# Weighted one-hot rows on GpSimd, and one filler product with VectorE sums in the step between layers

## The chip, the cores and the metric

The program runs on one core of a Trainium2 chip. A core has TensorE (matrix products, with its own weight loads), VectorE, ScalarE, GpSimd and SyncE, which here only issues DMAs. They run side by side and meet at semaphores. The metric is the device time of one execution in microseconds (us); lower is better.

## The reference

Two transformer blocks of two layers each, one after the other, on 256 tokens of width 1024, all in float32. This case touches two pieces.

The first block's feed-forward part is a product-key mixture (PEER), once per layer. Each token picks 16 of 16,384 experts in each of 8 heads, so 128 (expert, gate) pairs a token:

```python
def peer_ffn(h, w_q, sub_keys, u, v):
    scores = einsum('bshpd,hpnd->bshpn', (h @ w_q).reshape(b, s, 8, 2, 128), sub_keys)
    s1, i1 = top_k(scores[..., 0, :], 16); s2, i2 = top_k(scores[..., 1, :], 16)
    cand = s1[..., :, None] + s2[..., None, :]          # 256 candidates a head
    top, pos = top_k(cand, 16); gates = softmax(top)    # expert = (i1, i2) at pos
    act = gelu(einsum('td,ted->te', h, u[expert]))
    return einsum('te,ted->td', gates * act, v[expert])
```

The second block adds each sublayer's normed result, `x = x + g * rmsnorm(y, gain)`, and norms the new `x` again at the entry of the next sublayer.

## The kernel before

**The expert sublayer (`peer`).** No expert row is gathered. All 16,384 experts are treated densely, as 128 units of 128 experts (`KEYS` = 128), each a 128x1024 block of `u` that comes by DMA into a ring of 4 slots. For exact float32 products a unit is split into a high and a low part: ScalarE writes the high part (`high`, L2403), VectorE the low part (`low`, L2264), and TensorE multiplies 24 times (`hidden`, L2475) into PSUM. Three split buffers (`SPLITS`) tie them: ScalarE may make unit u's high part only when TensorE is done with unit u-3. ScalarE then applies the gelu (L2411) and SyncE stores the result.

In the same loop the routing is worked out. VectorE finds the top 16 in `top16` (max, max_index, match_replace) and turns the candidates into (first key, second key, gate) for the token half 1 and then for half 0. `pace()` puts a `low()` between the pieces of this work, five times in six. At the end of each half TensorE transposes the three lists (`turn`, L2483) and VectorE copies them to `selT` (L2385).

A dense table of gates, `G[key1, token, key2]`, is then built by products of one-hot rows. A batch is 4 tokens (`B` = 4), and there are 64 batches a layer. For each token VectorE makes a row `(iota == key1) * gate` (L2288, 4 instructions a batch) and, in one instruction for all four, `(iota == key2)` (L2291); TensorE multiplies each pair (`place`, L2493), and ScalarE copies the result into `G` (`take`, L2428). Both kinds of rows have two buffers, so batch n waits until `place(n-2)` is done. The order is fixed when the program is written: 16 batches of token half 1 are made between the routing steps of half 0 (`pace`, every second unit), the other 48 after both halves, one with each unit. TensorE's queue holds `hidden(j)`, then `turn` or `place` where VectorE's count says so, then `hidden(j+1)`.

**The step between sublayers of the second block (`add_streamed`).** It runs four times; in three of them (`counted`) it also sums the squares of the new `x`. TensorE sums the squares of `y` over partitions (L863), then multiplies seven times into a bank that nobody reads (L866, fillers), and widens the inverse roots (L869), which VectorE needs for `y * root` (L899) and `x + y` (L903), in four quarters. ScalarE squares each quarter (L916), and TensorE sums all the squares with 32 one-column products (16 with 256 columns; L876). At the next entry VectorE adds the four quarter sums (L144) and forms the root.

## Time and profile before

| | |
|---|---|
| three runs | median 3641.14 us (3630.91 to 3643.29) |
| the profiled execution | 3646.81 us, its span 3645.1 us |
| mean granted TensorE clock | 0.942 of full speed |
| TensorE busy | 3344.1 us, 92% |
| VectorE busy | 2173.9 us, 60% |
| ScalarE busy | 1453.5 us, 40% |
| GpSimd busy | 41.6 us, 1% |
| the expert sublayers' loop over `u` | about 455 to 890 us and 1480 to 1915 us |
| the four steps between sublayers | at 2794, 3207, 3388 and 3629 us |

The span runs from the first to the last instruction; the 1.7 us beside it lie around it. Busy shares are means over stages with different limits, so the place of an idle stretch and what ended it say more than the share. A `x4` in a row is several instructions in one; its time then runs from the first start to the last end, and instructions on one engine overlap a little at their ends.

### The profile page before, as it was taken

The numbers are of one execution on the slowest core, as the hardware profiler recorded it, in microseconds if no ns is written. First come the engines' busy times: TensorE is split into PE (matmuls) and PEld (weight loads), VectorE is DVE, ScalarE is ACT, GpSimd is POOL, SyncE is SP. The second block draws the span as 40 slices with busy tenths as digits, with TensorE's granted clock in tenths as the row PEclk, the third lists the DMA queues.
The fourth block names the chain that finished last, engine by engine and source line by source line (L and its number), as shares of the span: only waits on it lengthen the run. The fifth ranks groups of instructions, "written<-read, shape, count | busy, mean of one in ns | idle before, by whom it ended". The sixth has DMA issues, their size and how long they took to land. (4 is left out here: it accounts for less than half of the span.)

```text
span 3645.1 us, 54606 instructions
## 1 busy us (share of the span) xinstructions
PE 3344.1 (92%) x20704; PEld 2871.6 (79%) x20704; DVE 2173.9 (60%) x4205; ACT 1453.5 (40%) x2254; POOL 41.6 (1%) x66
## 2 busy tenths in 40 slices
PE   6987899999999798999999999799789999979897
PEld 4844799998888678999997887577556787867897
DVE  4523489875787635799767787423673443244553
ACT  3312444444455434444444544332233322233443
POOL 0000000000000000000000000000020000000000
PEclk7987999999999899999999999799897999979899
DMA  5465576556888635666567886322551232311353
GB/s 182 148 230 189 185 212 202 173 174 190 243 240 243 201 107 168 203 197 183 176 183 229 241 243 212 121 83 93 195 185 41 85 94 92 94 56 49 114 168 121
DMA packets 225066, 596.62 MB, mean 164 GB/s; under 512 B 27424, under 2 KB 97440, under 8 KB 224576
## 3 DMA queue, kind: packets, MB, share of 16 engines
q1 hardware_dynamic: 220656, 588.17, 52.6%
q10 hardware_dynamic: 4176, 5.29, 0.5%
q8 instruction: 152, 2.49, 0.3%
q14 instruction: 82, 0.67, 0.1%
HBM read 558.16 MB, written 35.19 MB: 163 GB/s over the span
## 5 line engine op out<-in xcount | busy, mean ns | idle before, releaser
L2475 PE MATMUL ps<-h_split,split_layer 128*128 128x256 f32 x6144 | 773.3, 285 | 11.0 <-DVE split_layer L2264 11.0
L2475 PEld LDWEIGHTS ps<-h_split,split_layer 128*128 128x128 f32 x6144 | 746.7, 192 | 14.3 <-DVE split_layer L2264 14.3
L2621 PE MATMUL ps<-split_layer,h_split 128*128 128x512 f32 x3072 | 702.3, 392 | 13.8 <-DVE h_split L2605 13.8
L2621 PEld LDWEIGHTS ps<-split_layer,h_split 128*128 128x128 f32 x3072 | 580.6, 189 | 135.1 <-DVE split_layer L2588 14.2
L784 PE MATMUL ps<-h_parts_ffn,split_ffn 128*128 128x512 f32 (+1 forms) x2112 | 381.6, 342 | 14.8 <-DVE split_ffn L736 8.2
L784 PEld LDWEIGHTS ps<-h_parts_ffn,split_ffn 128*128 128x128 f32 x2112 | 331.5, 193 | 65.8 <-issue 17.0
L2264 DVE TENSOR_TENSOR split_layer<-ring,split_layer 128x1024 fp32r<-128x1024 f32 x256 | 311.8, 1220 | 79.6 <-ACT split_layer L2403 77.9
L2588 DVE TENSOR_TENSOR split_layer<-ring,split_layer 128x1024 fp32r<-128x1024 f32 x256 | 313.7, 1226 | 0.0
L736 DVE TENSOR_TENSOR split_ffn<-ring,split_ffn 128x1024 fp32r<-128x1024 f32 x132 | 161.1, 1225 | 253.9 <-ACT split_ffn L711 245.9
L2411 ACT ACTIVATE kept_layer<-ps 128x256 f32<-128x256 f32 x256 | 98.3, 384 | 459.3 <-PE ps L2475 459.2
L2570 ACT ACTIVATE split_layer<-ring 128x1024 fp32r<-128x1024 f32 x256 | 267.6, 1045 | 4.5 <-PEq L472 4.5
L2403 ACT ACTIVATE split_layer<-ring 128x1024 fp32r<-128x1024 f32 x256 | 268.8, 1051 | 0.7 <-PEq L472 0.7
L2579 ACT ACTIVATE h_split<-x_sb 128x256 fp32r<-128x256 f32 x256 | 107.2, 419 | 350.2 <-PE ps L2621 345.8
L784 PE MATMUL ps<-hidden_ffn,split_ffn 128*128 128x512 f32 (+1 forms) x1056 | 189.4, 342 | 11.3 <-DVE split_ffn L736 11.3
L711 ACT ACTIVATE split_ffn<-ring 128x1024 fp32r<-128x1024 f32 x132 | 136.0, 1056 | 150.2 <-PE ps L784 125.0
L2605 DVE TENSOR_TENSOR h_split<-x_sb,h_split 128x256 fp32r<-128x256 f32 x256 | 109.2, 427 | 141.5 <-ACT h_split L2579 141.5
L784 PEld LDWEIGHTS ps<-hidden_ffn,split_ffn 128*128 128x128 f32 x1056 | 166.2, 194 | 34.5 <-issue 10.7
L2288 DVE TENSOR_SCALAR x_sb<-small 128x128 f32<-128x128 f32 x512 | 142.8, 343 | 84.7 <-PE ps L2493 84.6
L2597 DVE TENSOR_TENSOR x_sb<-x_sb,routes_layer 128x256 f32<-128x256 f32 x256 | 161.0, 629 | 21.4 <-DMA x_sb<-hidden_layer 21.4
L784 PE MATMUL ps<-h_parts_recurrent,split_recurrent_in 128*128 128x512 f32 x576 | 135.3, 396 | 9.3 <-DVE h_parts_recurrent L280 8.1
L784 PEld LDWEIGHTS ps<-h_parts_recurrent,split_recurrent_in 128*128 128x128 f32 x576 | 108.8, 190 | 36.2 <-issue 7.3
L2493 PE MATMUL ps<-x_sb 128*128 128x128 f32 x1024 | 136.9, 277 | 0.0
(612 smaller groups left out, 3891.1 us busy)
## 6 DMA issues: line engine op xcount, KB each, us to landing
ring<-in_experts SPq DMA_DIRECT2D x512, 512.0 KB, 3.9
ring<-in_mod SPq DMA_DIRECT2D x96, 512.0 KB, 4.6
ring<-in_ada SPq DMA_DIRECT2D x96, 512.0 KB, 4.4
ring<-in_ffn_in SPq DMA_DIRECT2D x88, 512.0 KB, 3.5
hidden_layer<-kept_layer SPq DMA_DIRECT2D x256, 128.0 KB, 2.0
x_sb<-hidden_layer SPq DMA_DIRECT2D x256, 128.0 KB, 3.9
ring<-in_ffn_out SPq DMA_DIRECT2D x44, 512.0 KB, 3.6
ring<-in_peer_q SPq DMA_DIRECT2D x32, 512.0 KB, 3.6
```

Of the source, the lines that this page charges most:

```text
L711: nc.scalar.activation(split[:, s % slots, 0, :], self.slot(u0 + s), ACT.Copy).then_inc(hi_done.sem, 1)
L736: nc.vector.tensor_tensor(split[:, s % slots, 1, :], self.slot(u0 + s), split[:, s % slots, 0, :].bitcast(F32), ALU.subtract).then_inc(sel ...
L784: ins = nc.tensor.matmul(ps[:, m % BANKS, 0:n], a, b, start=(k == 0 and j == 0), stop=(k == kt - 1 and j == 2))
L2264: v.tensor_tensor(split[:, u % SPLITS, 1, :], self.slot(unit0 + u), split[:, u % SPLITS, 0, :].bitcast(F32), ALU.subtract).then_inc(self.u ...
L2288: v.tensor_scalar(row1(half, j), self.iota, sel[:, 0, t:t + 1], sel[:, 2, t:t + 1], ALU.is_equal, ALU.mult)
L2403: s.activation(split[:, u % SPLITS, 0, :], self.slot(unit0 + u), ACT.Copy).then_inc(hi_done.sem, 1)
L2475: ins = nc.tensor.matmul(ps[:, 4 + j % 2, 0:T], w[:, part, c], self.hsplit[:, moving, k, :], start=(k == 0 and n == 0), stop=(k == KT - 1 ...
L2493: ins = nc.tensor.matmul(ps[:, n % 2, j * P:(j + 1) * P], row1(n % 2, j), row2(n % 2, j), start=True, stop=True)
L2570: s.activation(split[:, u % SPLITS, 0, :], self.slot(unit0 + u), ACT.Copy).then_inc(hi_done.sem, 1)
L2588: v.tensor_tensor(split[:, u % SPLITS, 1, :], self.slot(unit0 + u), split[:, u % SPLITS, 0, :].bitcast(F32), ALU.subtract).then_inc(self.u ...
L2597: v.tensor_tensor(raw(j), held(j), G[:, :, j:j + 1].rearrange("p t o -> p (t o)"), ALU.mult).then_inc(weighed_j.sem, 1)
L2621: ins = nc.tensor.matmul(ps[:, 2 * t + h, :], wsplit(j, a)[:, t * P:(t + 1) * P], w[:, b, h * 512:(h + 1) * 512], start=(j == 0 and n == 0 ...
```

## The change

In `peer`, the four weighted rows of a batch are no longer made by VectorE. GpSimd makes them, all 64 batches in a queue of its own: it waits for the list of the half (a semaphore of its own, raised by VectorE's copy to `selT`), and from the third batch on for `place(n-2)`. VectorE still makes the `(iota == key2)` rows of all four tokens, at the same places. TensorE's `place(n)` waits for both. In `add_streamed` one filler stands where seven stood; in the counted steps three fillers come after the last squares, VectorE adds the eight blocks of squares to one (four instructions), and TensorE's 32 (or 16) one-column products become 4 (or 2). The entry no longer adds quarter sums.

```diff
@@ class Norm, vector_root @@
-        if self.counted:
-            v.tensor_reduce(self.root, ps[:, 5, 16:16 + 4 * self.nt].rearrange("p (i t) -> p t i", t=self.nt), AX_X, ALU.add
-                            ).then_inc(done.sem, 1)
-            dve.wait_ge(done.sem, done.up())
-            v.tensor_scalar(self.root, self.root, 1.0 / D, EPS, ALU.mult, ALU.add).then_inc(done.sem, 1)
-        else:
-            v.tensor_scalar(self.root, ps[:, 5, 0:self.nt], 1.0 / D, EPS, ALU.mult, ALU.add).then_inc(done.sem, 1)
+        at0 = 16 if self.counted else 0
+        v.tensor_scalar(self.root, ps[:, 5, at0:at0 + self.nt], 1.0 / D, EPS, ALU.mult, ALU.add).then_inc(done.sem, 1)
@@ add_streamed, TensorE @@
-                for i in range(7):
-                    mm(ps[:, 7, 0:T], self.ones, total[:, 0:T], start=True, stop=True)
+                mm(ps[:, 7, 0:T], self.ones, total[:, 0:T], start=True, stop=True)
...
                 if counted:
-                    for i in range(QUARTERS):
-                        pe.wait_ge(self.squared.sem, at[self.squared] + i + 1)
-                        for t in range(nt):
-                            for k in range(per):
-                                ins = mm(ps[:, 5, 16 + i * nt + t:17 + i * nt + t],
-                                         squares[:, i * per + k, t * P:(t + 1) * P], self.ones[:, 0:1],
-                                         start=(k == 0), stop=(k == per - 1))
+                    pe.wait_ge(self.squared.sem, at[self.squared] + QUARTERS)
+                    for i in range(3):
+                        mm(ps[:, 7, 0:T], self.ones, total[:, 0:T], start=True, stop=True)
+                    pe.wait_ge(folded.sem, at[folded] + QUARTERS)
+                    for t in range(nt):
+                        ins = mm(ps[:, 5, 16 + t:17 + t], squares[:, 0, t * P:(t + 1) * P], self.ones[:, 0:1],
+                                 start=True, stop=True)
@@ add_streamed, VectorE, at the end of round i of the quarters @@
+                    if counted and i >= 3:
+                        dve.wait_ge(self.squared.sem, at[self.squared] + i - 1)
+                        if i > 3:
+                            dve.wait_ge(folded.sem, at[folded] + i - 3)
+                        a, b = fold(i - 2)
+                        v.tensor_tensor(a, a, b, ALU.add).then_inc(folded.sem, 1)
+                if counted:
+                    dve.wait_ge(self.squared.sem, at[self.squared] + QUARTERS)
+                    dve.wait_ge(folded.sem, at[folded] + QUARTERS - 2)
+                    a, b = fold(QUARTERS - 1)
+                    v.tensor_tensor(a, a, b, ALU.add).then_inc(folded.sem, 1)
+                    dve.wait_ge(folded.sem, at[folded] + QUARTERS - 1)
+                    v.tensor_tensor(squares[:, 0, :], squares[:, 0, :], squares[:, 1, :], ALU.add).then_inc(folded.sem, 1)
@@ peer, the loop over u @@
+            @block.gpsimd
+            def _(pool):
+                for n in range(BATCHES):
+                    half, b = n % 2, BATCH_ORDER[n]
+                    if n % (BATCHES // 2) == 0:
+                        pool.wait_ge(chosen.sem, chosen.n + n // (BATCHES // 2) + 1)
+                    if n >= 2:
+                        pool.wait_ge(placed.sem, placed0 + n - 1)
+                    for j in range(B):
+                        t = b * B + j
+                        ins = nc.gpsimd.tensor_scalar(row1(half, j), self.iota, sel[:, 0, t:t + 1], sel[:, 2, t:t + 1],
+                                                      ALU.is_equal, ALU.mult)
+                    ins.then_inc(weighted.sem, 1)
@@ onehot_rows, VectorE @@
-                    for j in range(B):
-                        t = b * B + j
-                        v.tensor_scalar(row1(half, j), self.iota, sel[:, 0, t:t + 1], sel[:, 2, t:t + 1],
-                                        ALU.is_equal, ALU.mult)
@@ the copy to selT, VectorE @@
-                                  ps[:, 6, 0:3 * P].rearrange("p (a b) -> p a b", a=3)).then_inc(done.sem, 1)
-                    after()
+                                  ps[:, 6, 0:3 * P].rearrange("p (a b) -> p a b", a=3)).then_inc(chosen.sem, 1)
+                    dve.wait_ge(chosen.sem, chosen.n + i + 1)
@@ place(n), TensorE @@
                     pe.wait_ge(onehots.sem, onehots0 + n + 1)
+                    pe.wait_ge(weighted.sem, weighted0 + n + 1)
```

VectorE's order in the later 48 batches of the first layer, before: one batch and one `low` a unit. `handover_k` is raised by `place`, `handover_a` by ScalarE's high part; `x_sb<-small` is a row made from the lists.

```order
L2288 TENSOR_SCALAR x_sb<-small 128x128 [waits handover_k]
L2288 TENSOR_SCALAR x_sb<-small 128x128 x3
L2291 TENSOR_TENSOR x_sb<-small 128x2x256
L2264 TENSOR_TENSOR split_layer<-ring,split_layer 128x1024 [waits handover_a]
L2288 TENSOR_SCALAR x_sb<-small 128x128 [waits handover_k]
```

The same place in the changed kernel, where L2320 is the row for four tokens and L2297 the low part:

```order
L2320 TENSOR_TENSOR x_sb<-small 128x2x256 [waits handover_k]
L2297 TENSOR_TENSOR split_layer<-ring,split_layer 128x1024 [waits handover_a]
L2320 TENSOR_TENSOR x_sb<-small 128x2x256 [waits handover_k]
L2297 TENSOR_TENSOR split_layer<-ring,split_layer 128x1024 [waits handover_a]
L2320 TENSOR_TENSOR x_sb<-small 128x2x256 [waits handover_k]
```

Four rows a batch are gone from VectorE, and its wait for `place(n-2)` has passed to the remaining row. GpSimd's order in the changed kernel, at the same place, with the rows in its own queue:

```order
L2285 TENSOR_SCALAR x_sb<-small 128x128 [waits handover_k]
L2285 TENSOR_SCALAR x_sb<-small 128x128 x3
L2285 TENSOR_SCALAR x_sb<-small 128x128 [waits handover_k]
L2285 TENSOR_SCALAR x_sb<-small 128x128 x3
```

TensorE keeps its order there; only the first product of a batch (L2524 in the changed kernel) has one more semaphore to wait for.

```order
L2524 MATMUL ps<-x_sb 128x128 [waits handover_l,weighted_rows,handover_j]
L2524 MATMUL ps<-x_sb 128x128 x3
L2504 MATMUL ps<-h_split,split_layer 128x256 [waits handover_c,unit_used]
L2504 MATMUL ps<-h_split,split_layer 128x256 x23
```

TensorE's order in the first of the four steps between sublayers, before:

```order
L863 MATMUL ps<-small,arena_block_layer 128x1 x4
L866 MATMUL ps<-arena_block_layer,small 128x256 x7
L869 MATMUL ps<-arena_block_layer,small 128x512
L876 MATMUL ps<-small,arena_block_layer 128x1 x32
```

and after the change:

```order
L859 MATMUL ps<-small,arena_block_layer 128x1 x4
L861 MATMUL ps<-arena_block_layer,small 128x256
L864 MATMUL ps<-arena_block_layer,small 128x512
L869 MATMUL ps<-arena_block_layer,small 128x256 x3
L873 MATMUL ps<-small,arena_block_layer 128x1 x4
```

Six fillers have left the place ahead of the widening product, three have come behind it, and 28 of the 32 one-column products are gone.

## Rows read from the trace of the kernel before

**Rows 1.** The page, busy time, share of the span and instructions.

```profile
PE 3344.1 (92%) x20704; PEld 2871.6 (79%) x20704; DVE 2173.9 (60%) x4205; ACT 1453.5 (40%) x2254; POOL 41.6 (1%) x66
```

**Rows 2.** Busy time by stretches: length, then engines' busy us, granted clock, DMA share, GB/s.

```profile
700.00:720.00 20.00, 20.00 (x172) 20.00 (x172) 15.34 (x31) 9.16 (x16) 0.00 (x0) 1.00 0.58 184
```

**Rows 3.** Timeline of one unit among the later batches: start, length, engine, line.

```profile
704.66 1.06 PE L2493 MATMUL ps<-x_sb 128*128 128x128 f32 x8
705.76 1.12 DVE L2288 TENSOR_SCALAR x_sb<-small 128x128 f32<-128x128 f32 x4 [0.91 <-PE ps L2493]
706.79 0.68 DVE L2291 TENSOR_TENSOR x_sb<-small 128x512 f32<-128x512 f32 x1
707.40 1.21 DVE L2264 TENSOR_TENSOR split_layer<-ring,split_layer 128x1024 fp32r<-128x1024 f32 x1
708.43 1.06 PE L2493 MATMUL ps<-x_sb 128*128 128x128 f32 x8
```

**Rows 4.** Timeline where the routing of half 0 ends, first layer.

```profile
665.32 1.23 DVE L2264 TENSOR_TENSOR split_layer<-ring,split_layer 128x1024 fp32r<-128x1024 f32 x1
666.46 1.12 DVE L2288 TENSOR_SCALAR x_sb<-small 128x128 f32<-128x128 f32 x4
666.60 3.14 PE L2475 MATMUL ps<-h_split,split_layer 128*128 128x256 f32 x24 [0.34 <-DVE split_layer L2264]
673.29 0.29 DVE L2379 TENSOR_TENSOR routes_layer<-routes_layer 128x128 f32<-128x128 f32 x1
673.64 0.90 PE L2483 MATMUL ps<-small,routes_layer 128*128 128x128 f32 x3 [3.90 <-DVE routes_layer L2379]
674.34 1.92 PE L2493 MATMUL ps<-x_sb 128*128 128x128 f32 x8
```

**Rows 5.** TensorE's turn, L2483: its idle time ahead, weight loads and products, both layers.

```profile
  DVE routes_layer L2379: 16.0, 4
```

**Rows 6.** Busy time of L2288 alone: length, VectorE busy (instructions), clock, DMA.

```profile
540.00:672.00 132.00, 17.78 (x64) 1.00 0.64 192
```

**Rows 7.** The page, ScalarE's high part: busy us, mean ns, idle before.

```profile
L2403 ACT ACTIVATE split_layer<-ring 128x1024 fp32r<-128x1024 f32 x256 | 268.8, 1051 | 0.7 <-PEq L472 0.7
```

**Rows 8.** GpSimd's instructions by form: busy us, mean ns.

```profile
L3099 POOL TENSOR_TENSOR arena_recurrent<-arena_recurrent,arena_block_layer 128x512 f32<-128x512 f32 x7 | 8.9, 1268 | 0.0
L1218 POOL TENSOR_SCALAR_AFFINE_SELECT small<-small 128x128 f32<-128x128 f32 x8 | 2.4, 300 | 0.6
```

**Rows 9.** Lines where GpSimd runs beside VectorE: min/median/max ns.

```profile
L1218 POOL TENSOR_SCALAR_AFFINE_SELECT arena_layer<-arena_layer x2: 1158/1158/1159, 55.5 to 56.7; 128x128 f32<-128x128 f32 x2
L1819 DVE TENSOR_TENSOR h_split<-h_layer,h_split x2: 1227/1270/1312, 54.0 to 55.2; 128x1024 fp32r<-128x1024 f32 x2
```

**Rows 10.** Timeline, the recurrent stage, VectorE beside GpSimd's L3100.

```profile
2620.44 1.75 DVE L3133 TENSOR_TENSOR arena_recurrent<-arena_recurrent,arena_block_layer 128x512 f32<-128x512 f32 x1
```

**Rows 11.** Timeline of the first step between sublayers.

```profile
2797.68 5.96 PE L866 MATMUL ps<-arena_block_layer,small 128*128 128x256 f32 x14
2798.50 0.87 DVE L891 TENSOR_SCALAR arena_block_layer<-small,arena_block_layer 128x128 f32<-128x128 f32 x4 [0.27 <-ACT arena_block_layer L910]
2803.48 1.02 PE L869 MATMUL ps<-arena_block_layer,small 128*128 128x512 f32 x2
2804.54 2.35 DVE L899 TENSOR_TENSOR h_block_layer<-h_block_layer,ps 128x1024 f32<-128x1024 f32 x2 [5.16 <-PE ps L869]
2809.17 13.81 PE L876 MATMUL ps<-small,arena_block_layer 128*128 128x1 f32 x64 [4.67 <-ACT arena_block_layer L916]
2812.59 2.19 ACT L916 ACTIVATE arena_block_layer<-x_sb 128x1024 f32<-128x1024 f32 x2 [1.21 <-DVE x_sb L903]
2825.91 0.17 DVE L144 TENSOR_REDUCE entry_ffn<-ps 128x4 f32<-128x16 f32 x1
```

**Rows 12.** Busy time by stretches, the fillers of the same step.

```profile
2800.00:2802.00 2.00, 2.00 (x6) 1.64 (x5) 0.00 (x0) 0.00 (x0) 0.00 (x0) 0.50 0.00 0
```

**Rows 13.** VectorE's L899, its idle time ahead over all four steps.

```profile
  PE ps L869: 16.2, 4
```

More of the change, by code:

```diff
@@ L436, in __init__ @@
          self.l) = (sig(f"handover_{x}") for x in "abcdefghijkl")
+        self.gates_chosen, self.weighted_rows = sig("routes_chosen"), sig("weighted_rows")
         self.kept = [sig(f"hidden_kept{i}") for i in range(2)]
@@ L852, in add_streamed @@
         x = self.xT[:, :, c0:c1]
-        scaled, summed = self.a, self.c
+        scaled, summed, folded = self.a, self.c, self.e
         counts, inverted, rooted, diagonals, widened = (self.entry_counted, self.inverted, self.rooted, self.diagonals,
@@ L857, in add_streamed @@
         per = KT // QUARTERS
-        at = {s: s.n for s in (scaled, summed, counts, inverted, rooted, diagonals, widened, self.squared)}
+        at = {s: s.n for s in (scaled, summed, folded, counts, inverted, rooted, diagonals, widened, self.squared)}
         with self.block() as block:
@@ L896, in _ @@
                 part = lambda i: slice(i * per, (i + 1) * per)
+                fold = (lambda i: (squares[:, part(0), :], squares[:, part(i), :])) if counted else None
                 for i in range(QUARTERS + 1):
@@ L920, in add_streamed @@
         if counted:
-            self.squared.up(QUARTERS)
+            self.squared.up(QUARTERS), folded.up(QUARTERS)
         self.arena.at = mark
@@ L2253, in peer @@
         gate_at, found_at, place_at = [], [], []
+        chosen, weighted = self.gates_chosen, self.weighted_rows
+        weighted0 = weighted.n
         with self.block() as block:
+            @block.gpsimd
[11 more added lines that the diff above has]
+                    ins.then_inc(weighted.sem, 1)
             @block.vector
@@ L2527, in peer @@
             x.up(TT)
-        for x in (onehots, placed, taken):
+        for x in (onehots, placed, taken, weighted):
             x.up(BATCHES)
+        chosen.up(TT)
         for x in self.kept:
```

## Prediction

> **What bounds the kernel now.** I read the page's busy times first: TensorE is busy for 92% of the span, GpSimd for 1% [rows 1]. So a change on VectorE or GpSimd is worth only what TensorE waits for them, and that is read stage by stage. Next the busy time by stretches. Where the later batches are made TensorE is busy for 20.00 of 20 us and VectorE for 15.34 [rows 2]. The timeline of one unit there says the same: `place` starts at 704.66 and again at 708.43, a period of 3.77 us; VectorE finds its buffer free only when a `place` ends, after 0.91 us idle [rows 3]. VectorE waits for TensorE, not the reverse. Then the end of the routing of half 0: VectorE is never idle, TensorE waits 0.34 and then 3.90 us for it, and the eight records of the `place` behind the last wait take 1.92 us where they take 1.06 in the steady state [rows 3, 4]. The second layer has the same last wait: the four idle times (weight loads and products, two layers) add to 16.0 us [rows 5]. Last the step between sublayers, which is a serial chain: whatever leaves it shortens the program. Its fillers run at half the granted clock, 1.2 GHz [rows 12].
>
> **Part 1, the rows leave VectorE, later batches (48 a layer).** VectorE loses four instructions, 1.03 us from the first start to the start of L2291 [rows 3]. TensorE has no wait there, so this is worth nothing; TensorE's 3.77 us hide it. VectorE keeps 0.68 and 1.21 us a unit [rows 3].
>
> The added wait is TensorE's, for GpSimd's rows. Behind it in TensorE's queue stands the next `hidden`, and behind that everything. GpSimd is released by `place(n-2)`, at 705.72, and its rows are wanted by `place(n)`, one unit after 708.43, at 712.2: 6.5 us. Over many batches it must keep to 3.77 us for four instructions. No row shows this instruction on GpSimd. The nearest is a select over 128x128 with one tensor input, 0.30 us; the far end is a 128x512 sum with two, 1.27 us [rows 8]. Mine has the small shape, but two operations and two per-partition scalars: I take 0.5 us, near the first, so 2.0 us a batch.
>
> It also meets VectorE. Beside back-to-back low parts of the same shape as L2264, GpSimd's select took 1.158 instead of 0.30 us: it got in only between VectorE's instructions. VectorE's instruction took 1.312 instead of 1.227 us, 0.085 more [rows 8, 9]. With two inputs of 512 elements GpSimd held up VectorE longer: L3133, a 128x512 sum that takes 0.68 us beside nothing, took 1.75 [rows 10]. So one side waits while the other reads, and a read of 128 elements is short. In a unit, then: GpSimd's first instruction ends behind L2291, at about 0.8 us, the second behind L2264, at 2.0, and two free ones at 3.0: under 3.77. TensorE's period then stays. If no part of GpSimd's work overlapped VectorE's 1.9 us, the batch would take 3.9: 0.13 us over, 6 us in 48 batches, of which the 2.7 us in hand (6.5 less 3.77) absorb part. I take nothing; the ends are 0 and 7 us later over both layers.
>
> The Trainium skill (SBUF — State Buffer, section Who interferes with whom) says that a VectorE instruction with two SBUF inputs and a GpSimd instruction that reads SBUF exclude each other, and that the second blocks fully. The trace agrees for GpSimd's wait [rows 9]; for VectorE it shows a price of 0.085 us, not of an instruction. The sum by the rule taken whole is my third rival.
>
> The skill's GPSIMD Engine Reference (section Engine selection) puts GpSimd at about half VectorE's speed for two-input elementwise work and near its speed for one input. By it the four rows would take an estimated 1.4 to 2.7 us, which fits in 3.77 and changes no term.
>
> **Part 2, the same in the routing of half 0 (16 batches a layer, 64 instructions [rows 6]).** Here VectorE is the late one. A batch frees 1.03 us and GpSimd costs at most 4 x 0.085 = 0.34, net 0.7; 16 batches give 11 us. VectorE can't use them all, since the low part of unit u needs the high part, and that needs `hidden(u-3)` to be over. How far ahead must it be? After its last low part ahead of the `turn` (665.32 + 1.23 = 666.55) VectorE works until 673.58 [rows 4]; 7.0 less 0.7 is 6.3 us, and TensorE needs 3.1 for that unit's `hidden`, so a lead of 3.2 us at 666.55 closes the gap. The greatest lead is two `hidden` and a `place`, 2 x 3.1 + 1.06, less what stands between the end of `hidden(u-3)` and the low part of u: a gelu, 1.05 for the high part [rows 7] and 1.21 [rows 3], in all about 2.9. That is 4.4 us, enough by 1.2 if lumps of 2.3 us in VectorE's work don't use it up. TensorE then gains 0.34 + 3.90 and the slow restart, 1.92 - 1.06 = 0.9: 5.1 a layer, 10.3 for both [rows 4, 5]. I take 10; the ends are -31 (VectorE loses, the third rival) and 11. The first rows are early: GpSimd may start them at the copy to `selT`, ahead of VectorE's next search. Here GpSimd has two units a batch (over 6.6 us), so a wait behind a 2.3 us instruction is covered. No DMA is moved; the fetch of a unit follows its low part, a few us earlier, with TensorE still behind.
>
> **Part 3, six fillers leave (four steps).** In the first step seven fillers take 5.96 us from 2797.68, though VectorE's diagonals are ready at 2798.50 + 0.87 = 2799.37 [rows 11]. One filler takes 0.85 and ends before them. So VectorE's wait ahead of L899, 5.16 us there and 16.2 over the four steps [rows 11, 13], shrinks to the widening product: 1.02 us for 512 columns after the clock had risen [rows 11], twice that at 1.2 GHz, half that for 256 columns. Without fillers I expect the low level in the two wide steps: 2.1 + 2.1 + 1.0 + 0.9 = 6.1. Gain 10.1 us; with all four at the low level 9.4, at the high level 12.5.
>
> **Part 4, sums of squares (three steps).** First step, counted from the start of L899 at 2804.54. Before: L876 ends at 2822.98, 18.4 us. After: the last square, 10.2 us in [rows 11], moves by one VectorE addition, 1.13, to 11.4. Two more additions on VectorE end at 13.3; the three fillers, at 0.85, end at 13.9 and decide; 8 records of 64, 13.81/8 = 1.7, end at 15.7. Gain 2.7, and the same in the second. In the third everything but the fillers is half as long: 9.2 before, 5.7 + 2.6 + 0.9 = 9.2 after, nothing. Together I take 5 us. With fillers at the high clock 1.3 us a step and half the products go too, up to 10; were the additions slower than the fillers, 2.
>
> **Part 5.** L144 and the wait behind it go from the entry chain, 0.2 us three times [rows 11]: 0.6.
>
> **Sum.** 10 + 10.1 + 5 + 0.6 = 25.7 us. The profiled execution took 3646.8 (span 3645.1), 5.7 over the median of the runs; it would take 3621. From the median, 3641.1 - 25.7 = 3615.
>
> **Rivals.**
> - *GpSimd sets the pace* (slower). For: one half of the bounds lies there; the instruction has no row. It decides from 0.47 us an instruction without any overlap with VectorE, from 0.94 with full overlap (3.77/4). Priced at 0.9 us with half of VectorE's 1.9 us in the way: 4.55 a batch, 0.78 over, times 48, less 2.7 in hand: 35 us a layer, 70 in all. The routing's gain goes as well: 70 - 15.7 = +54, 3695. Against: 0.30 us for the nearest form. Chance 0.10.
> - *The routing's gain doesn't come*, because VectorE's lead is used up in lumps or TensorE waits for GpSimd's rows there. Gain 15.7 to 18: 3624. For: the margin is 1.2 us against lumps of 2.3. Chance 0.15.
> - *Each GpSimd instruction holds VectorE up for its whole 0.5 us.* Then a batch in the routing costs VectorE 2.0 against 1.03 freed: 16 us later a layer, 31 in all, and the later batches 3.9 us each, some 7. 38 - 15.7 = +22: 3663. For: L3133 was held up for 1.07 us [rows 10]. Against: 0.085 for the small shape. Chance 0.04.
> - *The clock.* The fillers that leave are TensorE's only wide work in the step, and its entry and first products then run at 1.2 GHz for some us longer. Four places at 2 to 4 us: gain 10 to 16, 3628. Against: at 2809 to 2823 TensorE was busy with L876 and the next products started at the low level already. Chance 0.15, of which 0.06 falls within 0.3%.
> - *Nothing to be told apart*, by small losses at each wait: 3640. Chance 0.04.
>
> **How the numbers follow.** The forecast has 0.52; its own range is 3603 to 3623: with every part at its good end the sum is 34 us, 3607, and the runs before spread over 12 us. 0.3%, 11 us, is about what a measurement of this kernel can tell from no change. Faster: 0.52 + 0.15 + 0.09 = 0.76. Within: 0.06 + 0.04 = 0.10. Slower: 0.14. The range runs from 3603 to 3644; it leaves out the slower cases and a little below.
>
> **What would show it.** Right: GpSimd's rows near 0.5 us between VectorE's, 2 to 3.1 us a batch; the period in the later batches still 3.77; TensorE's wait ahead of L2483's successor for half 0 under 0.8 instead of 3.90; VectorE's waits ahead of `y * root` adding to about 6 instead of 16.2; 15.7 from there to the last one-column product in the first step. Wrong: a period over 3.8 with TensorE waiting for GpSimd, VectorE's L2264 longer by more than 0.1 us each, or a granted clock of half speed for longer behind the steps.

## The result: slower by 1.1%

The changed kernel takes 3680.45 us (median of 3 runs, 3675.05 to 3680.94) against 3641.14: ratio 1.0108, 95% interval 1.0087 to 1.0130. The forecast was 3615 in a range of 3603 to 3644, a gain; it became a loss. The profiled execution took 3680.94 us, its span 3679.2, mean granted clock 0.946.

### The profile page after: what moved, and what is told of

Same layout as the page of the kernel before. It is cut to its first block and busy times, and to the rows that moved or that the text cites. A ratio compares the mean times of both kernels' runs of the same rounds, so it can differ in the third digit from the quotient of the medians.

```text
span 3679.2 us, 54287 instructions
## 1 busy us (share of the span) xinstructions
PE 3323.3 (90%) x20534; PEld 2839.4 (77%) x20534; DVE 2057.6 (56%) x3702; ACT 1453.5 (40%) x2254; POOL 622.0 (17%) x578
## 5 line engine op out<-in xcount | busy, mean ns | idle before, releaser
L2285 POOL TENSOR_SCALAR x_sb<-small 128x128 f32<-128x128 f32 x512 | 580.3, 1147 | 899.7 <-DVE small L2414 823.9
L780 PE MATMUL ps<-h_parts_ffn,split_ffn 128*128 128x512 f32 (+1 forms) x2112 | 381.9, 342 | 15.9 <-DVE split_ffn L732 8.2
L2297 DVE TENSOR_TENSOR split_layer<-ring,split_layer 128x1024 fp32r<-128x1024 f32 x256 | 313.1, 1225 | 109.3 <-ACT split_layer L2432 108.0
L2320 DVE TENSOR_TENSOR x_sb<-small 128x512 f32<-128x512 f32 x128 | 88.5, 691 | 235.7 <-PE ps L2524 235.6
L780 PEld LDWEIGHTS ps<-hidden_ffn,split_ffn 128*128 128x128 f32 x1056 | 167.4, 195 | 34.1 <-issue 10.3
L2524 PE MATMUL ps<-x_sb 128*128 128x128 f32 x1024 | 142.5, 282 | 39.8 <-issue 39.8
L2524 PEld LDWEIGHTS ps<-x_sb 128*128 128x128 f32 x1024 | 125.3, 192 | 55.1 <-issue 55.1
```

The source lines that it names most:

```text
L780: ins = nc.tensor.matmul(ps[:, m % BANKS, 0:n], a, b, start=(k == 0 and j == 0), stop=(k == kt - 1 and j == 2))
L2285: ins = nc.gpsimd.tensor_scalar(row1(half, j), self.iota, sel[:, 0, t:t + 1], sel[:, 2, t:t + 1], ALU.is_equal, ALU.mult)
L2297: v.tensor_tensor(split[:, u % SPLITS, 1, :], self.slot(unit0 + u), split[:, u % SPLITS, 0, :].bitcast(F32), ALU.subtract).then_inc(self.u ...
L2524: ins = nc.tensor.matmul(ps[:, n % 2, j * P:(j + 1) * P], row1(n % 2, j), row2(n % 2, j), start=True, stop=True)
```

## The profile after

The page's busy times and two of its costliest groups, to be set beside [rows 1, 7]. The last column of a group is the idle time of the engine ahead of it.

```profile
PE 3323.3 (90%) x20534; PEld 2839.4 (77%) x20534; DVE 2057.6 (56%) x3702; ACT 1453.5 (40%) x2254; POOL 622.0 (17%) x578
...
L2285 POOL TENSOR_SCALAR x_sb<-small 128x128 f32<-128x128 f32 x512 | 580.3, 1147 | 899.7 <-DVE small L2414 823.9
...
L2524 PE MATMUL ps<-x_sb 128*128 128x128 f32 x1024 | 142.5, 282 | 39.8 <-issue 39.8
```

GpSimd took over 512 instructions and is busy 580 us more. TensorE now has 39.8 us of idle time ahead of `place` (L2524), with no instruction of the profile named for it ("issue"). What it waits for is seen among the later batches. Busy time by stretches, to be set beside [rows 2]:

```profile
700.00:720.00 20.00, 17.77 (x143) 17.10 (x144) 7.93 (x10) 9.07 (x15) 20.00 (x20) 1.00 0.48 143
```

GpSimd, the fifth of the busy columns, is busy for 20.00 of 20 us and TensorE no longer. The timeline of one unit, to be set beside [rows 3]:

```profile
699.52 11.24 POOL L2285 TENSOR_SCALAR x_sb<-small 128x128 f32<-128x128 f32 x11
...
704.86 1.13 PE L2524 MATMUL ps<-x_sb 128*128 128x128 f32 x8 [0.46 <-issue]
...
706.02 0.69 DVE L2320 TENSOR_TENSOR x_sb<-small 128x512 f32<-128x512 f32 x1 [2.62 <-PE ps L2524]
706.63 1.22 DVE L2297 TENSOR_TENSOR split_layer<-ring,split_layer 128x1024 fp32r<-128x1024 f32 x1
...
709.31 0.91 PE L2524 MATMUL ps<-x_sb 128*128 128x128 f32 x6 [0.45 <-issue]
```

`place` starts at 704.86 and 709.31: a period of 4.45 us instead of 3.77. GpSimd never stops, and VectorE idles 2.62 us a unit instead of 0.91. GpSimd is the engine with no slack. Its instruction by itself (min/median/max ns), over the later batches, and then the one that runs at 706.9 to 707.0 in the unit above:

```profile
L2285 POOL TENSOR_SCALAR x_sb<-small x117: 783/789/2150, 719.7 to 848.7; 128x128 f32<-128x128 f32 x117
L2285 POOL TENSOR_SCALAR x_sb<-small x1: 2147/2147/2147, 706.3 to 706.3; 128x128 f32<-128x128 f32 x1
```

Three of the four instructions of a batch take 0.79 us. One is 2.15 us long: it starts at 706.3, while VectorE's L2320 runs (from 706.02), and ends at 708.4, some 0.6 us behind the end of L2297 (707.85). It is held up for 2.15 - 0.79 = 1.36 us. Together 3 x 0.79 + 2.15 = 4.5 us, the period of 4.45, since neighbours overlap a little.

The hidden products of each layer give the length of the loop (first and last start stand ahead of the form). Before, then after, in both layers:

```profile
L2475 PE MATMUL ps<-h_split,split_layer x3072: 278/283/562, 443.0 to 885.8; 128*128 128x256 f32 x192
L2475 PE MATMUL ps<-h_split,split_layer x3072: 278/283/561, 1469.7 to 1912.6; 128*128 128x256 f32 x192
```

```profile
L2504 PE MATMUL ps<-h_split,split_layer x3072: 277/283/415, 435.8 to 904.5; 128*128 128x256 f32 x192
L2504 PE MATMUL ps<-h_split,split_layer x3072: 277/283/561, 1486.8 to 1958.1; 128*128 128x256 f32 x192
```

The first loop began at 443.0, not at about 455 as the table of before has it. The loops lasted 442.8 and 442.9 us and now last 468.7 and 471.3: +54.3 together. The steps between sublayers give back 14.0 (worked out below). The span grew by 34.1; the remaining -6.2 is mostly the time ahead of the first loop, which began at 443.0 before and at 435.8 after. No part of the change lies there, and in the kernels below that start varies from 429.6 to 443.7, so I don't count it as an effect of the change.

The end of the routing of half 0, to be set beside [rows 4]:

```profile
663.67 0.55 PE L2512 MATMUL ps<-small,routes_layer 128*128 128x128 f32 x3 [2.87 <-DVE routes_layer L2408]
664.05 1.06 PE L2524 MATMUL ps<-x_sb 128*128 128x128 f32 x8
```

The wait for the finished lists is 2.87 us, neither the old 3.90 nor the expected value under 0.8. The first step between sublayers, to be set beside [rows 11]:

```profile
2843.22 1.61 PE L859 MATMUL ps<-small,arena_block_layer 128*128 128x1 f32 x8 [2.48 <-PEq L468]
2844.69 1.20 PE L861 MATMUL ps<-arena_block_layer,small 128*128 128x256 f32 x2
2846.45 2.08 PE L864 MATMUL ps<-arena_block_layer,small 128*128 128x512 f32 x2 [0.55 <-DVE arena_block_layer L887]
2859.99 2.93 PE L869 MATMUL ps<-arena_block_layer,small 128*128 128x256 f32 x6 [11.47 <-ACT arena_block_layer L931]
2862.71 1.71 PE L873 MATMUL ps<-small,arena_block_layer 128*128 128x1 f32 x8
2865.06 3.78 PE L160 MATMUL ps<-x_sb,small 128*128 128x256 f32 x8 [0.65 <-DVE small L749]
2868.91 2.04 PE L181 MATMUL ps<-scaled_ffn,small 128*128 128x512 f32 x2
...
2873.86 1.32 PE L780 MATMUL ps<-h_parts_ffn,split_ffn 128*128 128x512 f32 x3 [2.91 <-DVE h_parts_ffn L278]
```

VectorE's `y * root` (L896) in that step, and then its idle time ahead over the four steps, to be set beside [rows 13]:

```profile
2848.56 2.35 DVE L896 TENSOR_TENSOR h_block_layer<-h_block_layer,ps 128x1024 f32<-128x1024 f32 x2 [2.17 <-PE ps L864]
```

```profile
  PE ps L864: 5.9, 4
```

The one filler ends at 2845.89, ahead of the diagonals. The widening product takes 2.08 us. VectorE's wait over the four steps fell from 16.2 to 5.9. From the start of L896 at 2848.56 to the end of the last one-column product at 2864.42 it is 15.9 us, where it was 18.4.

## The experiments

Theory A: GpSimd sets the pace of the later batches, by its own 0.79 us an instruction and by being held up behind VectorE's two-input instructions. There are two rivals: that TensorE's added wait and the longer chain cost the time, whatever GpSimd has to do; or that the step between sublayers is what lost. "Loops" below are the lengths of the two loops over `u`, read as above. All kernels were measured against the kernel before on the same chip (its medians: 3641.5 to 3644.5 us); intervals are 95%.

### The rows on GpSimd alone, and the step alone

gpsimd_only is the changed kernel with the old `add_streamed` and the old root at the entry; step_only is the kernel before with the new ones.

> The changed kernel with the step between sublayers and the entry's root as before: GpSimd's rows alone. Theory A (GpSimd sets the pace of the later batches: 0.79 us an instruction, one of four held up 1.36 us behind VectorE's two, 4.45 us a batch against 3.77): the two loops over u are 54 us longer, the rest is as before; 3641 + 54 = 3695 us, ratio 1.015. Theory B (the step between sublayers cost time, GpSimd's rows only a little): ratio under 1.005.

Measured: 3693.16 us, ratio 1.0130 (1.0107 to 1.0154); loops 471.6 and 470.2 us.

> The kernel before with the changed step between sublayers and nothing on GpSimd. Theory A: the step is faster by what its parts showed, some 16 us: 3625 us, ratio 0.9955. Theory B: slower than before, ratio over 1.003.

Measured: 3633.28 us, ratio 0.9966 (0.9950 to 0.9982), loops 442.7 and 443.8 us. So the whole loss is the rows', and the step is worth some 12 us (7 to 18). The sum of both, 1.013 x 0.9966 = 1.0096, is the changed kernel's ratio within its interval.

### GpSimd only in the routing

The first piece stands in GpSimd's queue, the second in VectorE's, the third in TensorE's.

```diff
-                for n in range(BATCHES):
+                for n in range(16):
...
+                    if n >= 16:
+                        for j in range(B):
+                            t = b * B + j
+                            v.tensor_scalar(row1(half, j), self.iota, sel[:, 0, t:t + 1], sel[:, 2, t:t + 1],
+                                            ALU.is_equal, ALU.mult)
...
-                    pe.wait_ge(weighted.sem, weighted0 + n + 1)
+                    if n < 16:
+                        pe.wait_ge(weighted.sem, weighted0 + n + 1)
```

> The changed kernel, but GpSimd makes only the 16 batches of a layer that fall into the routing; VectorE makes the rows of the other 48, as before. Theory A: the later batches are back at 3.77 us, the routing keeps what it gained (TensorE waits some 2.9 instead of 3.9 us ahead of its turn, and restarts without the slow place): 3641 - 16 - 5 = 3620 us, ratio 0.994. Theory C (any work that GpSimd does beside VectorE costs the loop): ratio over 0.9955, the step's gain alone.

Measured: 3622.95 us, ratio 0.9941 (0.9918 to 0.9963), loops 439.8 us both. With the 48 later batches back on VectorE the loss is gone. Against theory C the total alone doesn't decide, as its interval takes in 0.9955; the loops do, being 3.0 us shorter than before. That is the gain in the routing a layer, where the prediction had 5. The profile of this kernel shows why, in the low part's row over the routing (530 to 660 us), and what waited ahead of it:

```profile
L2297 DVE TENSOR_TENSOR split_layer<-ring,split_layer x39: 1199/1224/1389, 530.6 to 658.3; 128x1024 fp32r<-128x1024 f32 x39
...
  ACT split_layer L2437: 11.5, 15
```

VectorE waits 11.5 us, 15 times, for ScalarE's high part. In the kernel before it waited not once over the same stretch of the loop (543 to 672 us, as the loop began 13.4 us later). Its freed time is spent on waiting. By the order of the semaphores it is the three split buffers that cap its lead; no run here changes their number. Beside GpSimd the low part's median is 1.224 us, where before it was 1.217, so the 0.085 us that [rows 9] suggest is not paid each time, though the longest reached 1.389.

### Part of the rows on GpSimd

half_share gives GpSimd two of the four rows of every batch, three_share three; VectorE makes the others (`range(B)` becomes `range(2)` on GpSimd, and VectorE has a loop over `range(2, B)`; for three_share likewise with 3). All waits of the changed kernel stay.

> The changed kernel, but of the four rows of a batch GpSimd makes two and VectorE two. Theory A: GpSimd needs 2 x 0.79 + 1.36 = 2.9 us a batch, under 3.77, so TensorE sets the pace again: 3641 - 16 - 4 = 3621 us, ratio 0.994. Theory D (what costs is TensorE's additional wait for a second engine, 0.45 us idle ahead of each place, whatever GpSimd has to do): the period stays at 4.4 us, ratio 1.01.

Measured: 3621.98 us, ratio 0.9937 (0.9914 to 0.9960), loops 441.5 and 439.0 us.

> The changed kernel, but GpSimd makes three of the four rows of a batch and VectorE one. Theory A (time of a batch on GpSimd = number of rows x 0.79 us + 1.36 us held up behind VectorE): 3.73 us, just under TensorE's 3.77, so the loop is as fast as with two rows: first to last product of the first expert loop 439 to 444 us, ratio 0.993 to 0.996. If the held-up time grows with the number of rows (rows take turns with VectorE's instructions, 0.34 each), 3.4 us, the same. If TensorE's added wait itself cost, the period would be near 4.2 us and the loop near 460 us.

Measured: 3624.19 us, ratio 0.9948 (0.9930 to 0.9966), loops 440.2 us both. TensorE's `place` in half_share, then GpSimd and VectorE in one unit, and GpSimd's instruction over the later batches:

```profile
741.40 1.06 PE L2528 MATMUL ps<-x_sb 128*128 128x128 f32 x8
742.22 3.12 PE L2508 MATMUL ps<-h_split,split_layer 128*128 128x256 f32 x24
745.17 1.06 PE L2528 MATMUL ps<-x_sb 128*128 128x128 f32 x8
```

```profile
742.50 0.66 DVE L2321 TENSOR_SCALAR x_sb<-small 128x128 f32<-128x128 f32 x2 [1.38 <-PE ps L2528]
742.56 2.91 POOL L2285 TENSOR_SCALAR x_sb<-small 128x128 f32<-128x128 f32 x2 [0.85 <-PE ps L2528]
743.08 0.68 DVE L2324 TENSOR_TENSOR x_sb<-small 128x512 f32<-128x512 f32 x1
743.68 1.21 DVE L2297 TENSOR_TENSOR split_layer<-ring,split_layer 128x1024 fp32r<-128x1024 f32 x1
```

```profile
L2285 POOL TENSOR_SCALAR x_sb<-small x66: 862/1441/2065, 720.0 to 841.3; 128x128 f32<-128x128 f32 x66
```

In half_share the period is 3.77 us and TensorE has no wait, though it still waits for the semaphore of GpSimd's rows: the semaphore and the longer chain cost nothing, which rules the first rival out. It also parts the two prices. GpSimd's first instruction lies beside VectorE's one-input rows and takes 0.86 us, hardly more than 0.79. The second meets the two two-input instructions, from 743.08 to 744.89, and takes 2.07: it ends at 745.47, 0.58 us behind the second one's end. It was not let in at the seam between them (743.7), while the select of [rows 9] got in between two low parts; why they differ, no run here shows. With three rows GpSimd is at the edge: busy without a break, with the period still at 3.77 us (three_share):

```profile
740.00:760.00 20.00, 20.00 (x172) 20.00 (x171) 11.52 (x16) 9.09 (x15) 20.00 (x16) 1.00 0.54 167
```

### Shorter hold-up, shorter instruction

key_single is the changed kernel with VectorE's one two-input instruction for the four keys (L2320, 0.69 us) put back into four with one input each:

```diff
-                    v.tensor_tensor(rows2(half), iota4, column_key.unsqueeze(3).broadcast_to([P, B // 2, 2, P]),
-                                    ALU.is_equal).then_inc(onehots.sem, 1)
+                    for j in range(B):
+                        t = b * B + j
+                        ins = v.tensor_scalar(row2(half, j), self.iota, sel[:, 1, t:t + 1], None, ALU.is_equal)
+                    ins.then_inc(onehots.sem, 1)
```

> The changed kernel, but VectorE makes the four (iota == key2) rows with four instructions of one tensor input each in place of one instruction with two. GpSimd makes all four weighted rows. Theory A (only VectorE's instructions with two inputs in SBUF hold GpSimd up, and two of them back to back hold it up for their whole length): only the low part, 1.22 us, is left; the held-up time falls from 1.36 to 0.7 to 0.9 us, the period from 4.45 to 3.8 to 4.05 us, the loop from 469 to 445 to 452 us. Theory G (any VectorE instruction on SBUF holds it up): VectorE is busy for longer, the period grows to 4.8 us or more.

Measured: 3643.05 us, ratio 1.0001 (0.9988 to 1.0015); loops 451.7 and 450.6.

```profile
L2285 POOL TENSOR_SCALAR x_sb<-small x129: 783/989/1543, 719.7 to 849.5; 128x128 f32<-128x128 f32 x129
```

```profile
741.59 1.13 PE L2525 MATMUL ps<-x_sb 128*128 128x128 f32 x8
...
745.65 1.13 PE L2525 MATMUL ps<-x_sb 128*128 128x128 f32 x8
```

Period 4.06. GpSimd still makes all four rows; the longest took 1.54 instead of 2.15 us, 0.6 less, though others were stretched to 0.99. The expectation had put the period at 3.8 to 4.05 us; this is its far end. So 0.39 of the 0.68 us that the period had grown were the hold-up behind that one instruction, worth 17 and 21 us of the loops.

one_op leaves the gate multiplication out of GpSimd's instruction (`sel[:, 2, ...]` and `ALU.mult` become `None`), so its table of gates holds ones:

> The changed kernel, but GpSimd's instruction only compares (one per-partition scalar, one operation); the multiplication by the gate is left out, so the result is not the weighted one. Theory H (the instruction is long because of its second scalar and second operation): it falls from 0.79 to about 0.5 us, 4 x 0.5 + 1.36 = 3.4 us a batch, and the loop is back at TensorE's pace, 440 us, ratio 0.994. Theory I (the length is that of any such instruction on GpSimd): 0.79 stays, period 4.45, ratio 1.01.

Measured: 3619.08 us, ratio 0.9934 (0.9917 to 0.9952), loops 439.5 and 439.6 us.

```profile
L2285 POOL TENSOR_SCALAR x_sb<-small x136: 596/599/2047, 718.5 to 846.0; 128x128 f32<-128x128 f32 x136
```

The second operation with its own scalar costs 0.19 of the 0.79 us. Without it four rows just fit into the 3.77 us, with the hold-up no smaller (2.05 - 0.60 = 1.45). So the hold-up alone is borne. That 0.79 us an instruction alone would be borne too follows from 4 x 0.79 = 3.16 us, under 3.77; no run has it. Both together were not borne.

### One filler, nothing else

one_filler is the kernel before with `for i in range(7)` removed ahead of the filler, so that one is left.

> The kernel before with one filler in place of seven in the step between sublayers and nothing else. Theory A: VectorE's wait ahead of y * root falls from 16.2 to 6 us over the four steps; the rest of the step stays: 3641 - 10 = 3631 us, ratio 0.997. Theory J (the fillers pay for themselves through the clock): the products behind run at 1.2 GHz for longer and the gain is under 3 us, ratio over 0.999.

Measured: 3629.10 us, ratio 0.9963 (0.9946 to 0.9980), not to be told from step_only. Theory J (under 3 us) falls. The profiles part the two kernels. TensorE's timeline in its first and third steps (one filler stands at L865):

```profile
2791.71 1.62 PE L863 MATMUL ps<-small,arena_block_layer 128*128 128x1 f32 x8 [2.48 <-PEq L472]
...
2824.25 5.86 PE L784 MATMUL ps<-h_parts_ffn,split_ffn 128*128 128x512 f32 x12 [2.91 <-DVE h_parts_ffn L283]
...
3379.15 0.58 PE L863 MATMUL ps<-small,arena_block_layer 128*128 128x1 f32 x4 [1.63 <-PEq L472]
...
3384.52 6.99 PE L875 MATMUL ps<-small,arena_block_layer 128*128 128x1 f32 x32 [2.64 <-ACT arena_block_layer L915]
...
3398.38 3.85 PE L784 MATMUL ps<-h_parts_ffn,split_ffn 128*128 128x256 f32 x14 [1.73 <-DVE h_parts_ffn L283]
```

From the first product of the step to the first of the next matrix, in us (step 2 to the first entry product, step 4 to the end of the widening product), before, in one_filler and in the changed kernel:

| step | before | one filler | after |
|---|---|---|---|
| 1 | 35.6 | 32.5 | 30.6 |
| 2 | 33.0 | 30.9 | 27.9 |
| 3 | 21.7 | 19.2 | 19.2 |
| 4 | 4.1 | 2.7 | 2.7 |
| gain | | 9.1 | 14.0 |

The columns sum to 94.4, 85.3 and 80.4 us. Other profiles give the same: 94.7 in gpsimd_only with the old step, and within 0.1 of 80.4 in step_only and key_single with the new one.

### What kept the routing's gain small

TensorE's last wait there stayed at 2.87 us in the changed kernel and in early_gpsimd alike. more_low is early_gpsimd with one more low part ahead of VectorE's last long instructions of half 0; before_more_low is the kernel before with the same, and nothing on GpSimd.

```diff
                         after()
                         pace()
+                        if i == 1 and side == 1:
+                            low()
                         v.tensor_tensor(oh4, oh4, idxs[:, side].unsqueeze(2).broadcast_to(full), ALU.mult).then_inc(done.sem, 1)
```

> The kernel in which GpSimd makes only the rows of the 16 routing batches, with one more low part on VectorE in the last stretch of half 0's routing, ahead of the last multiplication by the expert lists. There TensorE waited 2.87 us for the finished lists (654.46 to 657.33), because VectorE worked from 651.3 to 657.2 without giving it a unit. Theory A (the lead is lumpy: what TensorE lacks is one more unit, not VectorE's time): the added low part takes 1.22 us, the lists are ready at 658.4 instead of 657.2, TensorE has 3.1 us more to do, so its wait falls from 2.87 to about 0.7, the loop from 439.8 to about 437.6 us a layer, the total by some 4 us to 3618, ratio 0.993. Rival B (VectorE's lead is capped by ScalarE's high part, or the sequence simply has too much VectorE work): the added low part waits, or TensorE waits elsewhere for the same time; loop 439.8, ratio 0.994. The two totals can hardly be told apart; the wait and the loop length in the profile decide.

> The kernel before with the same one more low part there, and nothing on GpSimd. Theory A: TensorE's wait ahead of the turn falls from 3.90 to about 1.9 us (hidden product until 672.9, lists at 674.8), the loop from 442.8 to about 440.8 us a layer, ratio 0.999, which a measurement of the total can't tell from 1. Rival B: loop 442.8. If A holds, two thirds of what GpSimd's rows gave in the routing (3.0 us a layer) were to be had by the order alone.

Measured: more_low 3617.76 us, ratio 0.9939 (0.9923 to 0.9955), loops 436.7 us both; before_more_low 3635.88 us, ratio 0.9986 (0.9975 to 0.9997), loops 441.1 us both. The totals can't tell the two theories apart; the profiles do. TensorE's wait ahead of the lists, in more_low and in before_more_low:

```profile
666.26 0.55 PE L2519 MATMUL ps<-small,routes_layer 128*128 128x128 f32 x3 [0.24 <-DVE routes_layer L2415]
```

```profile
675.52 0.55 PE L2485 MATMUL ps<-small,routes_layer 128*128 128x128 f32 x3 [1.28 <-DVE routes_layer L2381]
```

Some 6 us of work that VectorE does there without giving TensorE a unit (651.2 to 657.2 in early_gpsimd) caused the last wait. The order takes 2.6 us off it with the rows on GpSimd (2.87 to 0.24) and without (3.90 to 1.28); freed time on VectorE had taken 1.0 us off it. The loop became shorter by another 3.1 us on top of the 3.0 by rows on GpSimd, but by only 1.7 without them. The difference is the granted clock behind the wait, here by stretches in more_low and then in before_more_low:

```profile
664.00:668.00 4.00, 3.17 (x25) 2.73 (x25) 3.90 (x6) 1.82 (x3) 0.00 (x0) 1.00 0.10 37
676.00:680.00 4.00, 3.41 (x18) 3.35 (x18) 3.96 (x9) 0.09 (x1) 0.00 (x0) 0.63 0.56 143
```

At a clock of 1.00 the next 48 records of `hidden` take 6.02 us, at 0.63 they take 7.51.

### The pieces that help, together

combined is more_low with the old step and one filler.

> What the runs so far point to: GpSimd makes the rows of the 16 routing batches alone, VectorE has one more low part ahead of the last multiplication, and in the step between layers one filler stands where seven stood, with the 32 one-column products and the reduce of the kernel before (no sums on VectorE, no later fillers). Theory A (the step's gain is the fillers', 3629/3642; the sums on VectorE give nothing; the loop gives 5 us a layer): 13 + 10 = 23 us off, 3619, ratio 0.9935, as more_low or within 3 us of it. Rival (the sums on VectorE were worth their 5 us): 5 us slower than more_low, ratio 0.995.

Measured: 3620.64 us, ratio 0.9942 (0.9925 to 0.9959); loops 436.7 us both. It lies 2.9 us above more_low, in the direction of the rival's 5, which runs that spread over 14 and 15 us can't settle. The profiles settle it for the steps: combined needs 85.3 us in the four, as one_filler does, and more_low 80.3, so the sums on VectorE are worth some 4.9 us there, with the loops alike. more_low has the lowest median of all, 0.6% ahead of the kernel before; early_gpsimd, half_share, three_share, one_op and combined can't be told from it.

## Why the prediction was wrong, point by point

**What bounds the kernel** was right: TensorE without a wait in the later batches, VectorE late in the routing.

**Part 1 failed, and with it the sign.** The term that was put at nothing is GpSimd's pace in the later batches ("I take nothing"); it cost some 60 us over both layers. Two steps of the prediction led there. The first is "I take 0.5 us, near the first, so 2.0 us a batch". The second is "a read of 128 elements is short", from which two free instructions and two let in between VectorE's were to end at 3.0 us. The instruction takes 0.79 us, and it isn't let in between: one in four stands 1.36 us behind VectorE's pair. 3.16 + 1.36 = 4.5 us instead of 3.0. The prediction's other estimate for the four rows, 1.4 to 2.7 us, was below the 3.16 as well. The prediction knew both edges (0.47 us an instruction without any overlap, 0.94 with full overlap), and the truth lay between them: of VectorE's 1.83 us only 0.47 overlapped. The first rival, priced at 4.55 us a batch, had the mechanism and nearly the period, 4.45, though with 0.9 us an instruction and a hold-up of 0.95, where 0.79 and 1.36 were measured. Its +35 us a layer were 30.1, and its 3695 for the whole change, which gave up the routing's gain, was 15 us too high. A chance of 0.10 for it rested on the 0.30 us of another instruction alone. The nearest row, 0.30 us, is of a select with one input; taking a value near it for an instruction with two operations and two scalars was the choice that decided. The second operation alone costs 0.19 us, two thirds of that row's 0.30.

Over 48 batches 0.68 us are 32.6 us; less the routing's 3.0 and the 2.7 in hand that the prediction counted, 26.9. Measured: 25.9 and 28.4. By the starts of the units in the two traces the later batches lost 30.1 us in each layer (32.6 - 2.7 = 29.9), and the routing ahead of them had given back 4.2 us in the first and 1.7 in the second. The layers differ by the clock behind the last wait of the routing, as the last section shows.

**Part 2 had the mechanism, the size was off.** VectorE did get ahead, and GpSimd's neighbourhood cost it next to nothing (median 1.224 against 1.217 us). But the margin of 1.2 us was used up, as the second rival had it in part: 3.0 us a layer in early_gpsimd, not 5.1. The term is "enough by 1.2 if lumps of 2.3 us in VectorE's work don't use it up"; 11.5 us of VectorE's freed time were spent waiting for the high part. Of the 3.0, 1.8 came with the end of three short waits of TensorE for a low part (0.39, 0.42 and 0.34 us idle at 605.5, 663.1 and 666.6 us in the kernel before, 0.5 to 0.7 us each from unit to unit), of which the prediction counted only the last. The long wait of 3.90 us and the restart behind it, the bulk of the 5.1, gave only the other 1.2. The third rival (a whole instruction of hold-up for VectorE) fell.

**Part 3 held.** 10.3 us of waits went, where 10.1 were forecast; 9.1 reached the end of the steps with this edit alone. In the third step part of the gain was lost again: its one-column products ran 6.99 us instead of 5.97 without the fillers ahead of them.

**Part 4 held in its working, and Part 5 is inside it.** First step: 15.9 us against the forecast 15.7. Third: none against none. Both parts by the table: 14.0 - 9.1 = 4.9, where 5 and 0.6 were taken. The rival of the clock shows in one row of the first step: the entry's L181 took 2.04 us where its equal took 1.12 before. It isn't so each time: in the second step the same product took 1.12 us in the changed kernel and 2.08 in step_only.

**The sum by what was measured:** the 3646.8 us of the profiled execution of before, plus 54.3 for the loops, less 14.0 for the steps, is 3687. The run took 3680.9; the 6.2 us between them lie mostly ahead of the first loop.

## What to carry to other kernels

Work that moves to an idle engine is free only if its time per round, with the hold-up behind the other engine, is below the period of the bound engine. When no row shows the instruction, price it at the far end as well, and if that end crosses the period, move a part (with two of four rows on GpSimd the kernel was 0.6% faster, the step between sublayers included; four rows alone lost 1.3%). Relief of a late engine paid here only as far as its neighbour could follow; after that the order of its long pieces decided.

## What the runs showed of the hardware

GpSimd's 128x128 compare and multiply with two per-partition scalars takes 0.789 us, with the compare alone 0.599. A pair of such rows took VectorE 0.66 us in half_share, four in a row 1.12 us in the kernel before.

In the later batches the hold-up was one-sided. GpSimd beside VectorE's one-input rows took 0.86 us, and beside four of them up to 1.00 (key_single); beside two back-to-back instructions with two inputs it took 2.07, to 0.58 us behind the end of the second. VectorE's low part was not lengthened by it: medians 1.219 us before and after.

```profile
L2297 DVE TENSOR_TENSOR split_layer<-ring,split_layer x34: 1217/1219/1222, 702.2 to 849.1; 128x1024 fp32r<-128x1024 f32 x34
```

The hold-up grew with VectorE's chain of two-input instructions: behind the low part alone GpSimd's instruction took 1.54 us (key_single), behind two instructions 2.15. Behind three it took 4.05: in the routing of the changed kernel L2297, L2320 and L2397 run back to back from 656.25 to 660.41 us, and GpSimd's instruction that started at 656.9 ended at 660.9, past two seams:

```profile
L2285 POOL TENSOR_SCALAR x_sb<-small x1: 4046/4046/4046, 656.9 to 656.9; 128x128 f32<-128x128 f32 x1
```

The slow restart behind the last wait of the routing was the clock. Kernel before, then early_gpsimd, where TensorE had waited 3.90 and 2.87 us:

```profile
674.34:676.26 1.92, 1.92 (x10) 1.92 (x10) 1.92 (x3) 0.00 (x0) 0.00 (x0) 0.50 0.42 49
```

```profile
658.03:659.95 1.92, 1.92 (x10) 1.92 (x10) 1.92 (x3) 0.00 (x0) 0.00 (x0) 0.50 0.24 66
```

The granted clock was 0.50, 1.2 GHz, and `place` took 1.92 us. After the 0.24 us wait in more_low the clock over 664 to 668 us was 1.00. The fall isn't certain each time. In the changed kernel TensorE waited 2.87 us in the first layer and 2.88 in the second; the clock behind them was this:

```profile
664.00:668.00 4.00, 4.00 (x36) 4.00 (x35) 3.97 (x5) 0.00 (x0) 2.79 (x2) 1.00 0.54 146
1714.00:1718.00 4.00, 3.39 (x16) 3.39 (x17) 3.91 (x7) 0.00 (x0) 0.68 (x1) 0.50 0.22 48
```

`place` took 1.06 us in the first layer and 1.91 in the second, and the second gained 2.5 us less in the routing. In half_share it was the other way round: waits of 3.40 and 3.38 us, a `place` of 1.92 and of 1.06 us. Why, no run here shows.
